# A one-layer hybrid decoder step: state rows loaded and transposed ahead of the first products, and two fewer unread products in the routing

## The reference, cut to what matters

```python
xn = _rmsnorm(x, norm1)
proj = xn @ w_in                                   # 1024 -> 7456
xc, new_conv = _causal_conv(lru_x, conv_buf, conv_w, conv_b)      # conv_buf: last 3 rows
P_prev = concatenate([prev[:, None], P[:, :-1]])                  # prev: state_shift
Pm = P + (P_prev - P) * mu
...
x = x + merged @ w_out
t = _rmsnorm(x, norm2)
p_top, g_idx = top_k(softmax(t @ rg + rgb), 1)
q, e_idx = top_k(softmax(le_g), 2)
h = silu(t @ wg[e]) * (t @ wu[e]);  y += comb[e] * (h @ wd[e])
```

## Time and profile before

| | |
|---|---|
| median of 3 runs | 773.6 us (772.8 to 777.58) |
| the profiled execution, own time | 777.41 us |
| its span | 775.5 us |
| TensorE busy | 747.2 us (96% of the span) |
| VectorE / ScalarE busy | 444.4 / 240.9 us |
| mean granted TensorE clock | 0.991 |

### The profile page before, as it was taken

One profiled execution on the slowest core, in us unless ns is written; L12 is line 12 of the kernel. 1 busy time (PEld: TensorE's weight loads), 2 busy tenths in 40 slices (PEclk: granted clock), 3 DMA queues, 4 the chain that ended last, 5 costly groups with the idle time before them and its releaser, 6 DMA issues.

```text
span 775.5 us, 18133 instructions
## 1 busy us (share of the span) xinstructions
PE 747.2 (96%) x7037; PEld 461.6 (60%) x7037; DVE 444.4 (57%) x1175; ACT 240.9 (31%) x593; POOL 61.2 (8%) x71
## 2 busy tenths in 40 slices
PE   5999999999999999999999999999899999999896
PEld 4566666666666666676666666455455555555442
DVE  4365677777777777767867865524523433223225
ACT  4224343352452552452443442231101001100014
POOL 3000000400000000000000000000122222222110
PEclk9999999999999999999999999998999999999999
DMA  9443152770160160261161474498799999999995
GB/s 248 121 115 102 29 140 69 146 203 21 27 192 14 43 185 7 64 167 27 41 164 27 145 276 143 132 422 323 306 413 418 422 416 418 420 419 420 419 392 201
DMA packets 117286, 160.06 MB, mean 206 GB/s; under 512 B 27718, under 2 KB 92032, under 8 KB 110824
## 3 DMA queue, kind: packets, MB, share of 16 engines
q1 hardware_dynamic: 100692, 147.57, 52.8%
q0 software_dynamic: 5760, 7.80, 3.9%
q10 hardware_dynamic: 10789, 4.06, 2.0%
HBM read 154.43 MB, written 15.73 MB: 219 GB/s over the span
## 4 chain that ended last, share of the span: by engine, by line
PE 89%; DMA 4%; ACT 2%; DVE 2%; issue 1%; SPq 1%; ACTq 1%; POOLq 0%; DVEq 0%
PE bank L820 24%; PE bank L1250 13%; PE bank L1257 6%; PE bank L1002 5%; PE bank L826 5%; PE bank L1082 4%; PE bank L1140 4%; DMA scratch<-in_exp_up 3%; PE bank L792 2%; PE bank L1289 2%; PE bank L944 2%; PE bank L935 2%; PE bank L1034 1%; PE bank L854 1%; PE bank L1109 1%
## 5 line engine op out<-in xcount | busy, mean ns | idle before, releaser
L820 PE MATMUL bank<-xnT,wall 128*128 128x320 f32 x656 | 194.7, 441 | 0.0
L820 PEld LDWEIGHTS bank<-xnT,wall 128*128 128x128 f32 x656 | 118.6, 190 | 45.1 <-issue 2.6
L708 POOL DMA_INDIRECT merged<-xn2d,gidx x15 | 15.5, 1035 | 516.9 <-DVE gidx L2199 408.3
L2243 DVE COPY vecs<-bank 128x512 f32<-128x512 f32 x32 | 22.1, 690 | 57.0 <-PE bank L1257 30.6
L2248 DVE TENSOR_TENSOR scratch<-bank,n 128x512 f32<-128x512 f32 x30 | 20.5, 687 | 48.7 <-PE bank L1250 45.1
L1002 PE MATMUL bank<-xnT,wall 128*128 128x320 f32 x128 | 47.9, 456 | 0.3
L1682 ACT ACTIVATE vecs<-bank 128x128 f32<-128x128 f32 x32 | 8.9, 277 | 116.3 <-PE bank L1250 116.3
L1250 PE MATMUL bank<-scratch 128*64 128x256 f32 x320 | 38.4, 395 | 2.9 <-DMA scratch<-in_exp_up 2.5
L1250 PE MATMUL bank<-vecs,scratch 128*64 128x256 f32 x352 | 40.6, 382 | 0.5 <-DVE scratch L2184 0.5
L1449 ACT ACTIVATE shared<-bank 128x256 f32<-128x256 f32 x32 | 12.3, 385 | 73.5 <-PE bank L820 66.8
L1082 PE MATMUL bank<-xnT,wall 128*128 128x320 f32 x112 | 33.1, 439 | 0.7
(11 more groups left out here) (439 smaller groups left out, 1365.5 us busy)
## 6 DMA issues: line engine op xcount, KB each, us to landing
wall<-in_w_in SPq DMA_DIRECT2D x58, 512.0 KB, 5.5
scratch<-in_exp_gate SPq DMA_DIRECT2D x10, 1024.0 KB, 13.5
scratch<-in_exp_up SPq DMA_DIRECT2D x10, 1024.0 KB, 16.0
vecs<-in_exp_gate SPq DMA_DIRECT2D x10, 1024.0 KB, 9.6
vecs<-in_exp_up SPq DMA_DIRECT2D x10, 1024.0 KB, 11.9
scratch<-in_exp_down SPq DMA_DIRECT2D x6, 1024.0 KB, 13.8
shared<-in_exp_gate SPq DMA_DIRECT2D x10, 512.0 KB, 14.4
shared<-in_exp_up SPq DMA_DIRECT2D x10, 512.0 KB, 15.8
```

The lines of the kernel that those rows point to most:

```text
L820: q = mm(tpbank(L, name), wbuf[name][:, k, :], xnT[:, k, :], start=(k == 0), stop=(k == KC - 1))
L2243: CP(ye[:, e % 2, :], bank[6 + e % 2][:]).then_inc(S("ye"), 1)
```

## The change

The three state loads on SP go ahead of the weights lx and ly. The function `states()` is split: the transposes of `strows` come between the fourth and the fifth group of x, and those of `shrows` and `murows` behind the transpose of the vectors, ahead of the first product. The vectors' transpose goes to bank 0, since bank 1 now takes the shift rows. The unread products ahead of the wait for `Mk` go from five to three; the one behind it stays.

```diff
@@ sync
-            sp.dma_start(wbuf["lx"][:], w_in[:, :, 5 * D:5 * D + 128]).then_inc(S("w_lx"), 16)
-            sp.dma_start(wbuf["ly"][:], w_in[:, :, 5 * D + 128:5 * D + 256]).then_inc(S("w_ly"), 16)
             sp.dma_start(shrows, a["state_shift"][0]).then_inc(S("st_in"), 16)
             sp.dma_start(strows[0:24, :], a["state_conv"].rearrange("o b j d -> (o b j) d")).then_inc(S("st_in"), 16)
             sp.dma_start(strows[24:32, :], a["state_lru"][0]).then_inc(S("st_in"), 16)
+            sp.dma_start(wbuf["lx"][:], w_in[:, :, 5 * D:5 * D + 128]).then_inc(S("w_lx"), 16)
+            sp.dma_start(wbuf["ly"][:], w_in[:, :, 5 * D + 128:5 * D + 256]).then_inc(S("w_ly"), 16)
@@ tensor
-            for j in range(6):
+            def first_rows_turned(j):
...
+            def conv_states():
+
+                pe.wait_ge(S("st_in"), 16 * 7)
+                for c in range(KC):
+                    tr(bank[2][:, 32 * c:32 * c + 32], strows[:, c * P:c * P + P], ident[0:32, 0:32])
+
+            def shift_states(c0, c1):
+
+                for c in range(c0, c1):
+                    w = min(P, RWKV - c * P)
+                    tr(bank[1][0:w, 8 * c:8 * c + 8], shrows[:, c * P:c * P + w], ident[0:8, 0:8])
+
+            for j in range(4):
+                first_rows_turned(j)
+            conv_states()
+            first_rows_turned(4)
+            first_rows_turned(5)
             pe.wait_ge(S("vec_in"), 16 * 6)
             pe.wait_ge(S("pool_dma"), 16 * 6)
-            tr(bank[1][:, 0:128], vrows[:], ident).then_inc(S("vecT"), 1)
-
-            def states():
-
-                pe.wait_ge(S("st_in"), 16 * 7)
-                pe.wait_ge(S("vecc"), 2)
...
+            pe.wait_ge(S("vecc"), 1)
+            tr(bank[0][:, 0:128], vrows[:], ident).then_inc(S("vecT"), 1)
+            shift_states(0, NMU)
+            tr(bank[2][:, 256:256 + NMU + KC], murows[0:NMU + KC, :], ident[0:NMU + KC, 0:NMU + KC]).then_inc(S("vecT"), 1)
...
-                if n == "ly":
-                    states()
+            pe.wait_ge(S("vecc"), 2)
             pe.wait_ge(S("const_in"), 16)
...
-            unread(bank[2][:], 5)
+            unread(bank[2][:], 3)
             pe.wait_ge(S("Mk"), 1)
@@ vector
-            CP(vT[:, KC:], bank[1][:, KC:128]).then_inc(S("vecc"), 1)
+            CP(vT[:, KC:], bank[0][:, KC:128]).then_inc(S("vecc"), 1)
```

## The result

| | before | changed |
|---|---|---|
| median, 19 runs each | 773.27 us (770.37 to 778.56) | 776.59 us (775.40 to 778.79) |
| ratio | | 1.0037, 95% interval 1.0023 to 1.0051 |
| profiled execution, own time / span | 777.41 / 775.5 us | 776.27 / 774.5 us |
| mean granted clock | 0.991 | 0.992 |

The changed kernel is 0.4% slower. The two profiled executions say the reverse (776.27 against 777.41): that of before was a long one, that of the changed kernel an average one. The comparison therefore also needs a profile of an average execution of before, which is the first experiment.

The account below looks back on a forecast made before the run. TensorE was taken as the bound, 89% of the chain. Start -0.9 and unread products -1.65 gave -2.55 us for the profiled execution (774.9); the median was put at -0.8, 772.8 us, range 770.0 to 776.8.

Parts of the forecast that it names:

- The wait for st_in: Between the fourth and fifth x groups: all loads landed by 11.1 us, TensorE there at about 11.4; cost taken as 0.
- rival C: At the x groups: TensorE waits at st_in for rows not landed; +1 to +2 us, chance 0.08.
- The clock at the start: First products: moved products may see less or more of the lower clock, -0.7 to +1.0 us; +0.2 taken.
- The unread products: Routing, ahead of Mk: five to three starts the counting products 1.65 us earlier; worth 0 where the clock is up.
- rival A: Routing: with three unread products TensorE idles and the clock falls in the dispatch products; +1.7 us there, 776.1 us, chance 0.18.
- The transposes' pace: 36 moved transposes ahead of the first product: 107 ns each, 3.85 us; first product 3.0 us later after slack.
- the other bound: Low bound for the 36 moved transposes: 62 ns each, 2.2 us; first product 1.4 us later.
- The fall behind the block: Lower clock at 27.1 to 30.5 us, behind the state transposes between ly and gl, expected gone: -1.7 us.
- The loads on SP, the tail: State loads first on SP cost 0; gains ahead of the experts' loads, before 546 us, should reach the end whole.

Follow-up runs that it names:

- the first experiment: The kernel before run once more with no edit: 773.16 us, ratio 0.9985; its profiled execution took 773.80 us.
- the states' own wait: Changed kernel with five unread products, the wait between x groups counting only the three state loads, murows waited for with the vectors: 774.34 us, ratio 1.0004.
- the last run above: Changed kernel with five unread products, plus two products that nobody reads ahead of the wait for all seven loads: 773.29 us, ratio 0.9996.
- the start alone: The changed kernel with five unread products again in place of three: 776.59 us, ratio 1.0036.
- the load order: The kernel before with only the three state loads on SP moved ahead of lx and ly: 774.69 us, ratio 1.0015.
- the wait alone: The kernel before with the new SP order and the wait for all seven loads ahead of the fifth x group, no transpose moved: 774.27 us, ratio 1.0005.
- The cut in two: The kernel before with 18 state transposes behind lx and 18 behind ly; run twice: 773.08 us, ratio 0.9984, then 771.97 us, ratio 0.9961.

## Why the prediction was wrong

The forecast was 0.8 us faster; the change is 3 us slower.

1. *The wait for st_in*, "all have landed by 11.1 ... Cost 0 to 0.5; I take 0": **the step that failed first.** It took the landing time of POOL's small loads (5.9 us) from a trace with the old order on SP. With the states ahead such a load takes 7.9 us, and murows released TensorE at 13.0, after a wait of 1.36 us. This is rival C, which had 0.08. Its price was too small as well: 1 to 2 us for the wait, but behind the wait the clock was low under transposes and products (14.8 to 21.6). Without the wait the start costs nothing that can be measured (1.0004), nor does it with work put into the wait (0.9996), nor does the wait without the moved transposes (1.0005). Together they give 1.0036. Cost and cause of the wait stand on these medians; single profiles scatter, and one without the wait (r at 33.24) started more slowly than the changed kernel's.

2. *The clock at the start*, "+0.2". The sum took the first products at the lower pace as given, since the earlier trace rows show them so. The other execution of before has the clock up before the first product. There the move has something to lose that the sum did not contain. The first r product comes at 32.75 against 30.97 where both executions have the clock up at 11.5 us, and at 34.19 against 32.58 where neither has: 1.6 to 1.8 us later, and 3.2 where only the changed one lacks it. These are pairs of single executions.

3. *The unread products*, "-1.65 us" in this execution and "worth 0" where the clock is up. That the cut gains it in the profiled execution is not shown: the stage takes 14.35 us before and 12.58 in the changed kernel, but also 12.58 with five products where the clock is up. In the changed kernel's own profile two more products at 0.42 us a record would have ended about 0.5 us behind Mk (an estimate: 535.48 + 4 x 0.42 = 537.2 against 536.6), so there the cut is worth about 0.5. Where the clock is up it is not 0: the 2.14 us of idle TensorE can be followed by a fall (1.0019 with three, 1.0032 with one; two of the three profiles that have such an idle stretch). That is rival A, with 0.18; the changed kernel's own profile doesn't show it. It was priced at +1.7 us; the run of it alone gives 0.0019 x 773.6 = +1.5, and its one profile +2.8. Not every fall in the routing comes from the cut: with five products it comes ahead of or within them in before (528.9), in the states' own wait (526.9) and in the last run above (527.3); in the changed kernel it comes at 530.3, ahead of them.

4. *The transposes' pace.* The forecast's 107 ns holds at the lower level (2.96 us for 27 in the start alone), and the other bound nearly, 64 ns, at the upper one (1.79 us for 27 in the run of the states' own wait, 13.07 to 14.79). Neither is a property of the place; the clock decides. So the Trainium skill's rule for loads, "TensorE: Matmul & The Clock Gate", section "LDWEIGHTS (loading the stationary operand)", agrees with the traces at the lower level and is too dear at the upper.

5. *The fall behind the block*, -1.7. Right where it happens, but the gain was not kept: it is there in both profiles of before, in that of the load order and in that of three unread products, and gone from there in the changed kernel, where the clock is low for 6.8 us ahead of it instead; with the states' own wait it comes at 14.9. Two more profiles with the whole block (one unread product; the wait alone) lack it, and in the first of them r comes at 29.36. So its mean worth is below 1.7 us. The cut in two is the one edit here that may have earned it.

6. *The loads on SP, the tail.* No weight was late. In the changed kernel the experts start 0.9 us earlier than in the long execution of before (547.68 against 548.57) and the span ends 1.0 us earlier; in before once more they start at 545.04 and the span ends at 772.0. From there to the end it is 226.8 to 227.0 us in all three, so what is gained ahead of them arrives, as said.

Putting numbers on an execution that is 3.8 us above the median was the root of 2 and 3: what the change took away was mostly time that the other executions had not spent, and what it put at risk was the state that they were in. The factors of the parts, 1.0036 x 1.0019 = 1.0055, are above the 1.0037 of both, though within the intervals. Whether a slow start makes the fall in the routing rarer stays open: it would take profiles of many executions. So does the share of executions that start slow (the clock not up by 13 us: three of nine profiles with the old list of the start, two of five with the new), and what decides it.

## What to carry to other kernels

Here small transposes and a short wait on TensorE cost less by their own time than by the clock behind them: look at the granted clock in the stretch behind the edit, in more than one execution, before pricing. A load put first in a queue can delay small loads of other queues too, as here by 2 us, so a wait that counts several loads should count only those that its user needs. A block of small work behind which the clock falls may be worth cutting in two between streams of products (0.3 us for the cut against 1.7 for the fall, where it comes); cutting it in eight cost more than it saved.

## What was not expected of the hardware

- The clock can be up before the first product: in eight of the twelve profiles of the experiments and in that of the changed kernel it rises at 11.2 to 12.7 us, behind the first transposes of x; in the others with the old list of the start only at 16.9 or 17.3, and in two with the new one at 22.9 and 23.3. The same 32 records take 8.88 us or 10.46 for it.
- A change between transposes and float32 products costs TensorE about 0.3 us when it comes every four transposes (1.08 us a step against 0.80 by the parts; 2.24 us over eight steps).
- DMAs of different queues are not independent: with 233 KB of state rows issued on SP from 2.3 us on, ahead of the weights and not behind them, a 4 KB load that GpSimd issued at 4 us took 7.9 to 8.3 us to land and not 5.7 to 6.2 (seven profiles each).
- The clock can fall with TensorE busy throughout: in the run of the states' own wait it is at the lower level from 14.9 to 18.3 us, behind 3.4 us of transposes that follow each other with no idle time in the timeline.
